# One step of a streaming encoder layer: the sample's right outputs by way of B22 and T3, P7 ahead of P6, a fifth raw place; in attention the sample's step third

## The chip, the cores and the metric

The kernel runs on one core of one Trainium2 chip, in one launch. The metric is the device time in microseconds; the time before is the median of three runs, 1524.59 us (1523.52 to 1526.95).

## The reference, cut to what matters

A prompt of 1024 rows (64 per chunk) and a sample of 64 rows with 2048 cached positions go through one layer:

```python
n = rms_norm(x, norm_attn_g); q, k, v (diff), q, k, v (stick) = split(n @ w_in)       # 1024 x 3072
s = q . k / 8 - slope[h] * |q_pos - k_pos|, visible where k_pos // 64 <= q_pos // 64   # 4 heads, 2 maps each
o_diff = rms(softmax(s[0]) @ v - lam * softmax(s[1]) @ v) * subln_g * (1 - lam_init)
z = q . k / 8; a = sigmoid(z) * prod of (1 - sigmoid(z)) over later visible k          # 8 heads of 64
h = x + concat(o_diff, a @ v) @ w_out
y = rms_norm(h + (silu(m @ w_gate) * (m @ w_up)) @ w_down, norm_final_g), m = rms_norm(h, norm_ffn_g)
```

D_MODEL is 1024 and the hidden width 2816, so w_down is 2816 x 1024. All is fp32. slope[h] is 2^-2, 2^-4, 2^-6, 2^-8. The outputs are y and the new k and v, for prompt and sample.

## The kernel before, in words

Each stage is a function with its own block, and each engine runs its own list of instructions in the order written; semaphores tie them. SP issues nearly all DMAs, in the order written, and a load that waits holds up those behind it. An fp32 matmul is made of three: both operands are split in a high and a low part (ScalarE or VectorE casts, VectorE or POOL subtracts), and high x high, high x low and low x high are accumulated.

Attention (`attend`). Eight units (four differential heads, then four pairs of stick-breaking heads) of SPU = 5 steps each, 40 steps x. In a unit four steps each take two prompt blocks of 128 rows (the p-th block and the (7-p)-th, nine blocks of keys together), one step takes the sample (2112 keys). Before, the sample's step is the fifth of each unit. In iteration i TensorE makes the scores of step i + 3, transposes the weights of step i and multiplies them with the values; for a stick-breaking step ScalarE takes sigmoids (L801), and VectorE makes the products with a scan over each row (`survive`, L977, for step i + 1), four scans for a prompt step, one of 2112 columns for the sample's. A group of four transpositions needs the scans of its rows. Every iteration also prepares pieces of the next unit's keys (L1080, L767, L868), and in stick-breaking units VectorE turns the values into differences of neighbours (`shift`, L989, seven pieces a unit, by the table `shift_at`). In iterations 32 to 37 VectorE casts the 16 pieces of w_out (L1000) and POOL subtracts their low parts (L747).

The distance tables: POOL's iota writes `near` (128 x 1024, L718) and `far` (128 x 2112, two of 64 rows, L722) as signed distances. VectorE takes the absolute value (L886 near, L892 far) and multiplies by 0.25 once for each differential unit (L899, L905). The far table's absolute value and first scaling stand at iteration 0, the near table's at iteration -5.

`mix` multiplies with w_out, adds x and norms. `feed` makes gate and up and multiplies them, in the hidden stage with seven products of half-sized matrices (L2233 to L2235), and then the down product, which this change is about.

Down product (in `feed`). The prompt's hidden values A (1024 x 2816) and w_down B are cut in 2 x 2 quarters: rows of A in two halves, the 2816 into even and odd tiles f of 128, columns of B in left and right. Seven products q = 0 to 6 of 512 x 1408 by 1408 x 512 are made, from sums of quarters of A (in `s_dram`, made by `sum_s`) and of B (in `t_dram`, by `sum_t`). Each result of four row blocks r (L2262 to L2264 in PSUM, six banks in turn) is added by VectorE to those of the four corners y11, y12, y21, y22 that it belongs to (`add_result`, L2128, table TAKEN_BY): two, four, one, one, three, two and one additions. An entry (q, k) is a 128 x 512 piece of A's sum and one of B's, for k of 11. Per entry SP loads both (L1801, L1810, 256 KB each) into one of RAWS = 4 raw places, ScalarE casts both (L1940, L1941), POOL makes A's low part (L1880), VectorE B's (`low_b`, L2109), in one of SLOTS = 12 slots. TensorE takes the k in three groups (4, 4, 3); in a group for each r three matmuls per k. A raw place is free when both low parts are done, a slot when the group of the entry 12 before is done by all r. From entry 10 on each entry's loads are followed by one of 16 loads of h (L1818, 256 KB), to which the corners are added.

The sample (64 rows) needs A times B in full. Its hidden values are loaded at once (`sample_raw`, 704 KB, at entry 14), split by ScalarE (L1945) and VectorE (L2113), and multiplied inside the products q = 1, 2 and 3, whose B pieces are B11, B21 and B22 as they are, ahead of the last r of each group (L2277 to L2281). B12 is in no product as it is, so before there are 11 half entries (EXTRA) with B12's rows and without A, placed behind each group of q = 1; they have two raw places of their own in the halves of `g_sb`, so that NE = 88 entries.

The final norms of the top half's four tiles and of the sample are placed at entries late in q = 5 (`norm_entry`), when y11 and y12 are complete; those of the bottom half come after the last product. The stores of y follow by SP.

## Time and profile before

| | |
|---|---|
| median of the runs | 1524.59 us |
| the profiled execution | 1528.52 us, its span 1526.7 us |
| TensorE busy | 1444.3 us (95%), granted clock 0.976 |
| VectorE, ScalarE, POOL busy | 896.1, 572.9, 492.7 us |
| DMA | 212.55 MB, mean 139 GB/s |

Times are from the start of the span. Attention goes from 312 to 667 us, the hidden stage to 1275.6, the down product from there to the end. Idle time of TensorE is what to read first; a busy TensorE is shown with matmuls whose ends overlap the next ones' starts, so the distance of starts is the measure.

### The profile page before, as it was taken

The numbers are of one execution on the slowest core, as the hardware profiler recorded it, in microseconds if no ns is written. First come the engines' busy times: TensorE is split into PE (matmuls) and PEld (weight loads), VectorE is DVE, ScalarE is ACT, GpSimd is POOL, SyncE is SP. The second block draws the span as 40 slices with busy tenths as digits, with TensorE's granted clock in tenths as the row PEclk, the third lists the DMA queues.
The fourth block names the chain that finished last, engine by engine and source line by source line (L and its number), as shares of the span: only waits on it lengthen the run. The fifth ranks groups of instructions, "written<-read, shape, count | busy, mean of one in ns | idle before, by whom it ended". The sixth has DMA issues, their size and how long they took to land. (4 is left out here: it accounts for less than half of the span.)

```text
span 1526.7 us, 24037 instructions
## 1 busy us (share of the span) xinstructions
PE 1444.3 (95%) x9360; PEld 1240.3 (81%) x9360; DVE 896.1 (59%) x1242; ACT 572.9 (38%) x1123; POOL 492.7 (32%) x376
## 2 busy tenths in 40 slices
PE   7999999969999999879968999999999999889998
PEld 6788888848887776558858999999999999668886
DVE  4520000078886787945558766666666677684484
ACT  4211111147877777522324222222222223444352
POOL 1323330010000001621225554444554445254453
PEclk9999999979999999979988999999999999999999
DMA  7243111163444555433312443344444346876563
GB/s 248 104 155 117 52 46 49 45 160 103 123 118 126 143 142 144 137 117 128 100 62 83 161 161 133 126 141 138 161 133 161 136 172 214 283 247 201 158 228 110
DMA packets 184871, 212.55 MB, mean 139 GB/s; under 512 B 19840, under 2 KB 126712, under 8 KB 183352
## 3 DMA queue, kind: packets, MB, share of 16 engines
q1 hardware_dynamic: 176136, 193.19, 39.4%
q10 hardware_dynamic: 8624, 17.83, 3.2%
q8 instruction: 75, 1.23, 0.3%
q14 instruction: 36, 0.29, 0.1%
HBM read 151.66 MB, written 59.31 MB: 138 GB/s over the span
## 5 line engine op out<-in xcount | busy, mean ns | idle before, releaser
L360 PE MATMUL ps_proj<-shared,nT_hi 128*128 128x512 f32 x384 | 152.6, 397 | 1.6 <-POOL shared L171 0.9
L361 PE MATMUL ps_proj<-shared,nT_hi 128*128 128x512 f32 x384 | 152.0, 396 | 0.0
L362 PE MATMUL ps_proj<-shared,nT_lo 128*128 128x512 f32 x384 | 150.6, 392 | 0.0
L268 DVE TENSOR_TENSOR staging<-ps_proj,staging 64x512 f32<-64x512 f32 x6 | 4.2, 694 | 214.5 <-ACT staging L203 214.5
L203 ACT COPY staging<-ps_proj 128x512 f32<-128x512 f32 (+1 forms) x54 | 31.7, 586 | 233.9 <-PE ps_proj L362 215.5
L1130 PE MATMUL ps_aT<-ident,z 128*128 128x128 f32 (+1 forms) x568 | 96.8, 287 | 6.4 <-DVE z L977 6.4
L810 ACT COPY aT<-ps_aT 128x512 f32<-128x512 f32 (+2 forms) x168 | 86.6, 524 | 33.0 <-PE ps_aT L1130 31.6
L171 POOL TENSOR_TENSOR shared<-w_raw,shared 128x512 fp32r<-128x512 f32 x40 | 59.4, 1521 | 112.9 <-DVE shared L241 112.9
L977 DVE TENSOR_TENSOR_SCAN z<-z,near 128x1024 f32<-128x1024 f32 (+7 forms) x64 | 92.1, 1485 | 0.0
L1875 POOL TENSOR_TENSOR shared<-staging,shared 128x512 fp32r<-128x512 f32 x43 | 64.4, 1503 | 85.6 <-ACT shared L1912 85.6
L1875 POOL TENSOR_TENSOR ring_more<-staging,ring_more 128x512 fp32r<-128x512 f32 x45 | 71.0, 1582 | 60.2 <-ACT ring_more L1912 60.1
L360 PEld LDWEIGHTS ps_proj<-shared,nT_hi 128*128 128x128 f32 x384 | 72.7, 189 | 19.5 <-POOL shared L171 2.2
L747 POOL TENSOR_TENSOR shared<-staging,shared 128x512 fp32r<-128x512 f32 x16 | 38.3, 2415 | 150.0 <-DVE shared L1000 150.0
L362 PEld LDWEIGHTS ps_proj<-shared,nT_lo 128*128 128x128 f32 x384 | 72.7, 189 | 16.2
L361 PEld LDWEIGHTS ps_proj<-shared,nT_hi 128*128 128x128 f32 x384 | 72.8, 190 | 14.7
L1130 PEld LDWEIGHTS ps_aT<-ident,z 128*128 128x128 f32 (+1 forms) x568 | 65.0, 143 | 23.2 <-issue 10.7
L2233 PE MATMUL ps_up<-parts_early,shared 128*128 128x272 f32 x264 | 77.1, 292 | 3.4 <-POOL shared L1875 3.4
L2233 PE MATMUL ps_up<-shared,ring_more 128*128 128x272 f32 x264 | 76.9, 291 | 3.3 <-DVE shared L2006 3.3
L1925 ACT COPY aux<-ps_up 128x544 f32<-128x544 f32 x22 | 13.5, 613 | 173.2 <-PE ps_up L2235 173.2
L2234 PE MATMUL ps_up<-parts_early,shared 128*128 128x272 f32 x264 | 77.1, 292 | 0.0
L2235 PE MATMUL ps_up<-parts_early,shared 128*128 128x272 f32 x264 | 76.8, 291 | 0.0
L2234 PE MATMUL ps_up<-shared,ring_more 128*128 128x272 f32 x264 | 76.8, 291 | 0.0
(298 smaller groups left out, 4477.1 us busy)
## 6 DMA issues: line engine op xcount, KB each, us to landing
staging<-s_dram SPq DMA_DIRECT2D x58, 256.0 KB, 3.5
staging<-in_w_gate SPq DMA_DIRECT2D x11, 1024.0 KB, 7.8
blocks<-in_w_up SPq DMA_DIRECT2D x11, 1024.0 KB, 5.3
blocks<-in_w_down SPq DMA_DIRECT2D x11, 1024.0 KB, 9.7
t_dram<-blocks SPq DMA_DIRECT2D x11, 1024.0 KB, 3.9
s_dram<-blocks SPq DMA_DIRECT2D x11, 1024.0 KB, 5.2
w_raw<-in_w_in SPq DMA_DIRECT2D x5, 2048.0 KB, 8.6
staging<-t_dram SPq DMA_DIRECT2D x34, 256.0 KB, 4.3
```

The lines of the kernel that those rows point to most:

```text
L171: nc.gpsimd.tensor_tensor(w_lo[g % 2][:, k], w_raw[:, g % 2, k], w_hi[g % 2][:, k].bitcast(F32), ALU.subtract).then_inc(w_lo_done, 1)
L360: nc.tensor.matmul(out, a_hi, b_hi, start=(k == 0), stop=False)
L361: nc.tensor.matmul(out, a_hi, b_lo, start=False, stop=False)
L362: last = nc.tensor.matmul(out, a_lo, b_hi, start=False, stop=(k == KD - 1))
L747: nc.gpsimd.tensor_tensor(t["wo_lo"][part], raw[:, slot_of(raw_of["wout", n])].rearrange("p a b -> p (a b)"), t["wo_hi"][part].bitcast(F32 ...
L810: last = nc.scalar.copy(aT[:, G % AT, 0:f], ps_aT[:, G % 2, 0:f])
L977: nc.vector.tensor_tensor_scan(back, back, mask[:, ::-1], 1.0, ALU.mult, ALU.max).then_inc(ready, 1)
L1130: last = nc.tensor.transpose(ps_aT[0:m, G % 2, k], z(x, at, m), t["ident"][:, :])
L1875: nc.gpsimd.tensor_tensor(w_lo, product_source(m)[0], w_hi.bitcast(F32), ALU.subtract).then_inc(w_lo_done, 1)
L2233: nc.tensor.matmul(res, w_hi[:, k], x_hi, start=(k == 0), stop=False)
L2234: nc.tensor.matmul(res, w_hi[:, k], x_lo, start=False, stop=False)
L2235: last = nc.tensor.matmul(res, w_lo[:, k], x_hi, start=False, stop=(k == HK - 1))
```

## The change

In attention the sample's step of a stick-breaking unit is the third of its unit instead of the fifth; those behind it are the third and fourth prompt step. The shift pieces come up to an iteration earlier. The absolute value of the distance tables is taken only where distances are negative (the last 128 columns of near, the last 64 of far), and the far table's first scaling moves from VectorE to POOL, behind the iotas.

In the down product the half entries go: NE = 77. The sample's right half is (A_even + A_odd) B22 + A_even (B12 - B22): the sum of the sample's even and odd tiles is made by VectorE into PSUM (`add_even_odd`), split like the rest, and multiplied in q = 3 (B22), and T3 = B12 - B22 (sign turned against before) is the B piece of the product now at q = 4. For this P7 stands at q = 4 and P6 at q = 5, so that y12 is complete only after q = 5, and the norms of the top tiles move into q = 6. g_sb is a fifth raw place for whole entries up to q = 4; then four places, and g is loaded at entry 59 instead of at q = 3's start. sample_raw is loaded at entry 10 instead of 14.

```diff
+    def sample_place(x):
+        return SPU - 1 if is_diff(x) else 2
     def is_sample(x):
-        return x % SPU == SPU - 1
+        return x % SPU == sample_place(x)
...
+        p = x % SPU - (1 if x % SPU > sample_place(x) else 0)
...
-            for j, i in enumerate((-2, -1, 0, 0, 1, 1, 2)):
+            for j, i in enumerate((-2, -1, -1, 0, 0, 1, 1)):
                 shift_at.setdefault(SPU * u + i, []).append((u, j))
...
+            pool.wait_ge(tables, 3)
+            nc.gpsimd.tensor_scalar(far[:], far[:], 0.25, 0.0, ALU.mult, ALU.add).then_inc(tables, 1)
...
             def near_distances():
-                nc.vector.scalar_tensor_tensor(near[:], near[:], -1.0, near[:], ALU.mult, ALU.max).then_inc(near_done, 1)
+                last = near[:, seq - P:]
+                nc.vector.scalar_tensor_tensor(last, last, -1.0, last, ALU.mult, ALU.max).then_inc(near_done, 1)
...
             def far_distances():
-                nc.vector.scalar_tensor_tensor(far[:], far[:], -1.0, far[:], ALU.mult, ALU.max).then_inc(far_done, 1)
+                last = far[:, past:]
+                nc.vector.scalar_tensor_tensor(last, last, -1.0, last, ALU.mult, ALU.max).then_inc(far_done, 2)
...
                     far_distances()
-                    far_slope(0)
...
-    SLOTS, RAWS, NBANK, AHEAD = 12, 4, 6, 10
+    SLOTS, RAWS, NBANK, AHEAD = 12, 5, 6, 10
+    entries = [(q, k) for q in range(NPROD) for k in range(NP)]
-    TAKEN_BY = (("y12", "y22"), ("y11", "y12", "y21", "y22"), ("y11",), ("y12",), ("y12", "y21", "y22"),
-                ("y21", "y22"), ("y21",))
+    TAKEN_BY = (("y12", "y22"), ("y11", "y12", "y21", "y22"), ("y11",), ("y12",), ("y21", "y22"),
+                ("y12", "y21", "y22"), ("y21",))
...
-            return last_group(4) + 6 + norm_order.index(i)
+            return last_group(5) + 6 + norm_order.index(i)
+        gains_at = entry_of[5, 0]
         def place(e):
-            return RAWS + k % 2 if q == EXTRA else (a_count[e] - 1) % RAWS
+            return e % RAWS if e < gains_at else (e - gains_at) % (RAWS - 1)
...
-            x = staging[:, s * D:(s + 1) * D] if s < 3 else aux[:, 0:D]
+            x = staging[:, s * D:(s + 1) * D] if s < 3 else aux[:, 0:D] if s == 3 else g_sb
...
-                if e == AHEAD + TT:
+                if e == AHEAD:
                     sp.dma_start(sample_raw, t["sample_dram"]).then_inc(sample_loaded, 16)
...
             def high_sample():
-                nc.scalar.copy(sample[:, :, 0:dec], sample_raw).then_inc(sample_hi_done, 1)
+                nc.scalar.copy(sample[:, 0:NF, 0:dec], sample_raw).then_inc(sample_hi_done, 1)
+                act.wait_ge(sample_summed, 1)
+                nc.scalar.copy(sample[:, NF:, 0:dec], sample_sum).then_inc(sample_hi_done, 1)
...
+            def add_even_odd():
+                nc.vector.tensor_tensor(sample_sum, pairs[:, :, 0], pairs[:, :, 1], ALU.add).then_inc(sample_summed, 1)
             def low_sample():
+                for j, (fs, x) in enumerate(((slice(0, NF), sample_raw), (slice(NF, None), sample_sum))):
...
                 low_b(e)
-                if e == SLOTS + 2:
+                if e == SLOTS + 1:
+                    add_even_odd()
+                if e == SLOTS + 3:
                     low_sample()
...
             def down_sample(q, k, j, first, final):
-                f = 2 * k + (1 if q in (2, 3) else 0)
+                f = (None, 2 * k, 2 * k + 1, NF + k, 2 * k)[q]
...
-                        if r == TT - 1 and q in (1, 2, 3):
+                        if r == TT - 1 and q in (1, 2, 3, 4):
...
-                                if q == 1:
-                                    down_sample(1, k, 0, k == 0, False)
-                                    down_sample(EXTRA, k, 1, k == 0, False)
-                                else:
-                                    down_sample(q, k, q - 2, False, k == NP - 1)
+                                down_sample(q, k, (q - 1) // 2, q % 2 == 1 and k == 0, q % 2 == 0 and k == NP - 1)
```

The rest of the diff follows from these: counts of semaphores without the half entries, A_PLACE and two signs (`sum_s`, `sum_t`) turned, the corners that the norms wait for.

## Rows read from the trace of the kernel before

**Rows 1.** Windows of the down product: busy us (instructions) of each engine, clock, DMA share, GB/s.

```profile
1362.60:1519.30 156.70, 156.70 (x691) 128.19 (x689) 88.10 (x91) 64.46 (x114) 76.38 (x63) 1.00 0.56 181
```

**Rows 2.** Timeline of TensorE: start, us, line, operation, [idle before <- releaser].

```profile
1275.61 0.39 PE L2262 MATMUL ps_up<-parts_early 128*128 128x512 f32 x1
...
1299.39 0.47 PE L2262 MATMUL ps_up<-shared 128*128 128x512 f32 x1 [0.47 <-DVE shared L2109]
...
1359.27 0.77 PE L2262 MATMUL ps_up<-shared 128*128 128x512 f32 x1 [2.35 <-DVE shared L2109]
...
1519.09 0.39 PE L2264 MATMUL ps_up<-parts_early 128*128 128x512 f32 x1
```

**Rows 3.** Chain that ended last, 1355 to 1362: start, length of the piece.

```profile
1360.89 0.43 PE ps_up L2262
```

**Rows 4.** Waits of TensorE in the down product: us, times, longest.

```profile
PE ps_up L2262 <- DVE shared L2109: 7.9, 7, 2.4
```

**Rows 5.** Timeline of SP's queue, first half of the down product.

```profile
1302.66 0.65 SPq L1818 DMA_DIRECT2D blocks<-h_dram  x1
1312.02 0.33 SPq L1810 DMA_DIRECT2D g<-in_w_down  x1
...
1329.41 0.33 SPq L1810 DMA_DIRECT2D g<-in_w_down  x1
```

**Rows 6.** Timeline of VectorE in the down product.

```profile
1305.97 1.37 DVE L2109 TENSOR_TENSOR parts_early<-staging,parts_early 128x512 fp32r<-128x512 f32 x1 [0.59 <-ACT parts_early L1941]
1308.57 1.63 DVE L2113 TENSOR_TENSOR part_late<-blocks,part_late 128x1408 fp32r<-128x1408 f32 x1 [1.22 <-ACT part_late L1945]
...
1355.76 2.47 DVE L2128 TENSOR_TENSOR blocks<-ps_up,blocks 128x512 f32<-128x512 f32 x4
...
1470.73 4.08 DVE L2146 SCALAR_TENSOR_TENSOR blocks<-blocks,rstd,g 128x1024 f32<-128x1024 f32 x1
...
1477.63 2.39 DVE L2109 TENSOR_TENSOR parts_early<-staging,parts_early 128x512 fp32r<-128x512 f32 x2
```

**Rows 7.** The tile far: operations, duration ns min/median/max, first and last start.

```profile
L905 DVE TENSOR_SCALAR far<-far x4: 1249/1250/1260, 339.4 to 437.3; 128x2112 f32<-128x2112 f32 x4
...
L977 DVE TENSOR_TENSOR_SCAN z<-z,far x4: 4542/4543/4544, 517.0 to 653.1; 128x2112 f32<-128x2112 f32 x4
L722 POOL IOTA far<- x2: 1889/1890/1891, 313.0 to 314.9; 64x2112 f32 x2
...
L892 DVE SCALAR_TENSOR_TENSOR far<-far x1: 2349/2349/2349, 337.0 to 337.0; 128x2112 f32<-128x2112 f32 x1
L734 POOL MEMSET far<- x1: 1857/1857/1857, 467.7 to 467.7; 128x2112 f32 x1
```

**Rows 8.** Timeline of TensorE in attention.

```profile
342.77 0.58 PE L1110 MATMUL ps_z<-shared 64*128 64x256 f32 x2 [3.84 <-DVE lowest L933]
...
650.46 1.12 PE L1130 MATMUL ps_aT<-ident,z 128*128 128x128 f32 x4 [5.54 <-DVE z L977]
```

**Rows 9.** Timeline of ScalarE at attention's end.

```profile
664.51 0.31 ACT L828 ACTIVATE o_sb<-ps_o,v_last 128x64 f32<-128x64 f32 x1 [0.83 <-PE ps_o L1159]
```

**Rows 10.** Timeline of ScalarE in the down product: casts behind their loads.

```profile
1298.69 0.62 ACT L1940 CAST shared<-aux 128x512 fp32r<-128x512 f32 x1 [0.85 <-DMA aux<-in_w_down]
...
1304.80 0.63 ACT L1940 CAST parts_early<-staging 128x512 fp32r<-128x512 f32 x1 [0.82 <-DMA staging<-in_w_down]
...
1307.16 1.37 ACT L1945 CAST part_late<-blocks 128x1408 fp32r<-128x1408 f32 x1 [1.22 <-DMA blocks<-sample_dram]
```

**Rows 11.** Groups of the down product, POOL: busy us, mean ns.

```profile
L1880 POOL TENSOR_TENSOR parts_early<-staging,parts_early 128x512 fp32r<-128x512 f32 x30 | 42.7, 1424 | 43.8 <-ACT parts_early L1940 43.7
```

**Rows 12.** The tile near: scalings.

```profile
L899 DVE TENSOR_SCALAR near<-near x4: 681/682/916, 316.4 to 422.7; 128x1024 f32<-128x1024 f32 x4
```

**Rows 13.** Groups by form, VectorE: 470 to 600, then 603 to 658.

```profile
L977 DVE TENSOR_TENSOR_SCAN z<-z,near 128x1024 f32<-128x1024 f32 x6 | 13.4, 2269 | 0.0
...
L977 DVE TENSOR_TENSOR_SCAN z<-z,near 128x1024 f32<-128x1024 f32 x2 | 6.6, 3325 | 0.0
```

More of the change, by code:

```diff
@@ L1544, in feed @@
     NG = len(GROUPS)
[L1545 to L1553 removed]
+    SLOTS, RAWS, NBANK, AHEAD = 12, 5, 6, 10
+    entries = [(q, k) for q in range(NPROD) for k in range(NP)]
     NE = len(entries)
[L1555 to L1558 removed]
+    TAKEN_BY = (("y12", "y22"), ("y11", "y12", "y21", "y22"), ("y11",), ("y12",), ("y21", "y22"),
+                ("y12", "y21", "y22"), ("y21",))
+    A_PLACE = (2, 0, 1, 5, 4, 3, 6)
     entry_of = {what: e for e, what in enumerate(entries)}
[L1560 removed]
     def steps_until(q, k):
[L1564 removed]
+        return (q * NG + k // 4 + 1) * TT
     def summed(name, q, r):
@@ L1662, in feed @@
             old = user_before(e)
-            raw_landed[e] = (0 if old is None else raw_landed[old]) + (16 if q == EXTRA else 32)
+            raw_landed[e] = (0 if old is None else raw_landed[old]) + 32
         def slot(e):
@@ L1702, in feed @@
         s_stored = sem("s_stored")
-        raw_loaded = [sem(f"raw_loaded4{i}") for i in range(RAWS + 2)]
+        raw_loaded = [sem(f"raw_loaded4{i}") for i in range(RAWS)]
         a_hi_done = sem("a_hi_done")
@@ L1792, in load_entry @@
                     old = user_before(e)
-                    if q != EXTRA:
-                        sp.wait_ge(a_lo_done, a_count[old])
+                    sp.wait_ge(a_lo_done, old + 1)
                     sp.wait_ge(b_lo_done, old + 1)
@@ L1797, in load_entry @@
                 landed = raw_loaded[place(e)]
-                if q != EXTRA:
-                    sp.wait_ge(hidden_stored, 48 * (k + 1))
-                    sp.wait_ge(s_stored, 16 * (k + 1))
-                    sp.dma_start(a_raw, t["s_dram"][A_PLACE[q], k]).then_inc(landed, 16)
+                sp.wait_ge(hidden_stored, 48 * (k + 1))
+                sp.wait_ge(s_stored, 16 * (k + 1))
+                sp.dma_start(a_raw, t["s_dram"][A_PLACE[q], k]).then_inc(landed, 16)
                 rows = [t["w_down"][f * P:(f + 1) * P] for f in (2 * k, 2 * k + 1)]
@@ L1806, in load_entry @@
                     sp.wait_ge(t_stored, 16 * (k + 1))
-                src = (t_even[:, left], rows[0][:, left], rows[1][:, left], rows[1][:, right], t_odd[:, right],
-                       t_even[:, right], t_odd[:, left], rows[0][:, right])[q]
+                src = (t_even[:, left], rows[0][:, left], rows[1][:, left], rows[1][:, right], t_even[:, right],
+                       t_odd[:, right], t_odd[:, left])[q]
                 sp.dma_start(b_raw, src).then_inc(landed, 16)
@@ L1889, in _ @@
             for e, (q, k) in enumerate(entries):
-                if q != EXTRA:
-                    low_a(e)
+                low_a(e)
                 for c, i in enumerate(norm_order[:TT + 1]):
@@ L1938, in high @@
                 a_hi, _, b_hi, _ = slot(e)
-                if q != EXTRA:
-                    nc.scalar.copy(a_hi, raw(e)[0]).then_inc(a_hi_done, 1)
+                nc.scalar.copy(a_hi, raw(e)[0]).then_inc(a_hi_done, 1)
                 nc.scalar.copy(b_hi, raw(e)[1]).then_inc(b_hi_done, 1)
@@ L2201, in _ @@
                         add_result(q, r)
-                    if q == 3 and r == TT:
+                    if q == 4 and r == TT:
                         add_sample()
```

53 lines of the change are left out of this document (21 added, 32 removed).

## The prediction

> **What bounds the kernel now.** I read the page's busy line, then TensorE's waits by stage, then TensorE's timeline, then the queue and engine feeding each wait. TensorE is the bound; other engines matter where it waits. A microsecond taken from such a wait comes off the end if TensorE is busy from there on.
>
> Down product: TensorE does 7 x 11 x 4 x 3 = 924 matmuls and 11 x 4 x 2 = 88 for the sample, 1012. In the last 156.7 us it never waits: 156.70 us for 691, a spacing of 0.2268 us [rows 1]. The first of the 1012 starts at 1275.61, the last at 1519.09 [rows 2], so 243.5 us pass for 1011 spacings, which would need 229.3: 14.2 us are lost. All are lost before 1362.6. One is the wait for the eleventh entry (1299.39, idle 0.47), 0.6 us beyond its spacing. The longest is at 1359.27, idle 2.35, and behind it six matmuls come 0.43 apart [rows 2, 3], the 1.2 GHz level, for 1.2 us more. VectorE's low parts (L2109) end them: 7.9 us of idle in 7 waits [rows 4]; the restart behind each makes up much of the rest.
>
> What makes the low parts late: SP issues in order. At 1302.66 it has issued two of the half entries (the 11 loads of B12's rows, EXTRA) into their two places; the third waits for the first's low part until 1312.02 [rows 5]. For 9.4 us nothing is loaded, the full entries behind least of all. The same happens again up to 1329.41. Then q = 1's four-corner additions, 2.47 us per row block, fall between low parts that are already late at 1355.76 [rows 6], and give the two waits at 1356 to 1359.
>
> Attention, start: VectorE makes the far table at 337.0, 2.35 us absolute value (L892) and 1.25 us scaling (L905), with score reads queued behind; TensorE idles 3.84 us up to 342.77 for a bank [rows 7, 8]. Attention, end: VectorE's scans bound. TensorE idles 5.54 us up to 650.46; the last scan starts at 653.1 and takes 4.54; the last output starts at 664.51 [rows 7 to 9].
>
> **The change part by part. Half entries.** Off go 11 loads of 256 KB, 11 casts, 11 low parts; TensorE's count stays 1012. The two long pauses of SP go with their places. Loads can then be four to five entries ahead instead of blocked. I place what is late next:
> - Eleventh entry: its load waits for the last stored sums, as before; 0.6 us stays.
> - q = 1 starts at 1306.3 (1275.61 + 132 x 0.2268 + 0.7 of the first wait) and needs its fourth entry (e = 14) 9 matmuls later, at 1308.3. Before, e = 11 landed at 1298.7 and e = 14 at 1304.80, 2.04 us each (with the h load); the sample's 704 KB came behind, and with one h load (960 KB) took 2.36 [rows 10]. Now they go ahead of e = 11: 704/960 x 2.36 = 1.7 us later, so e = 14 lands at 1306.5. Casts to 1307.6. Low part 1.37 at 1305.97 [rows 6], and the new addition add_even_odd (128 x 704) stands ahead of it, which is nearest to half of the 1408 wide difference of 1.63: 0.8, behind e = 13 at 1307.4, so to 1308.3. Done at about 1309.7: wait 1.4. Bounds: 0 (addition inside the casts' time, the extra raw place brings loads forward), 2.4 (addition behind a POOL operation of 1.42 [rows 11]).
> - Sample's parts: needed 36 matmuls after the start, 1306.3 + 1.4 + 8.2 = 1315.9. Behind e = 14 on VectorE: an addition of two corners (half of 2.47), e = 15 (1.4), differences 1.63 + 0.8: 1314.8, or 1316.2 with one POOL operation ahead. 0.2 taken, bounds 0 and 1.
> - e = 18, with three more additions of two corners (1.24) and low parts (up to 1.37) ahead: about 1323.0 against a need at 1322.5. 0.4 taken, bounds 0 and 1.5.
> - q = 1 to 2: the additions (2.47 x 4) now stand at e = 23 to 26. With T the start of q = 2, the first row block is ready at T - 7.5, added by T - 5.0; each further pair (1.37 + 2.47) brings e = 24 to T - 3.6, e = 25 to T + 0.3 against a need at T + 2.0. Nothing, bound 1.5.
> - Half-clock stretch: goes, as no wait reaches 2.35.
> Left: 0.6 + 1.4 + 0.2 + 0.4 = 2.6 of 14.2, and 0.6 for restarts: **11.0 us** gained, bounds 7 (all upper bounds) and 12.9 (0.6 and 0.7 left).
>
> **P7 ahead of P6.** Three-corner additions move from q = 4 to 5, and the norms of the top rows from q = 5 to 6, with their stores. Nothing is added to the end: those rows follow the same adds in the same pattern. In q = 5 before, that pattern kept VectorE full (one norm took 4.08 us beside POOL), yet q = 5's last low parts ended at about 1478.7 to 1480 from 1470.73 and 1477.63 [rows 6], and q = 5 starts at 1519.3 - 2 x 29.9 = 1459.5, so its last entry is needed 23.2 later, at 1482.7. Slack near 4 us. Five y stores, 2.3 MB, in the last product end before its 29.9 us do. Cost 0, bound 2. Signs, A_PLACE and the gain's place and load: same instructions, 0. The fifth place ends at q = 5; q = 2 to 6 never waited with four.
>
> **Tables.** The far absolute value covers 64 columns instead of 2112 (0.2 instead of 2.35), and the first scaling (1.25) leaves VectorE: 3.4 us off a wait of 3.84, TensorE near full behind it. **3.4** taken; 1 if TensorE's next dependence (the combine's weights) comes right behind. The near absolute value loses 1.0 us or so, but the scaling behind it took 0.92 against 0.68 for its sisters while POOL's iota ran to 316.8 [rows 7, 12], and it would wait for that iota still: 0 taken, bounds 0 and a gain of 0.5. POOL's new scaling of 2112 columns lies between the memset of as many (1.86) and four differences of 512 (4 x 1.42 = 5.7) [rows 7, 11]; nearest to the memset, 2 to 3 us at 316.9 to 320, its reader comes 30 us later. Cost 0.
> The row shows a VectorE scaling held up while POOL runs. The Trainium skill says why, in SBUF - State Buffer, section "SBUF: two separate sides": VectorE and GpSimd share a port pair, and whoever starts first has it for the whole instruction. By that rule the new POOL scaling, if it starts ahead of near_slope, holds it for its whole length; the trace agrees so far as 0.92 against 0.68 goes.
> For that scaling the Trainium skill's GPSIMD Engine Reference, section "3.1 Elementwise", gives 1.03 cycles an element for light bodies, an estimate of 1.8 us; the sum would be the same.
>
> **Sample third, shifts earlier.** In the last unit the last step becomes a prompt step. VectorE is bound from about 606. Its scans from x = 34 on: before 4.5 + 4 x 5.3 + 4.5; after one of the two sample steps is a prompt step of about 5.3: +0.8. POOL's differences of w_out delay scans by 1.05 each (1024 wide: 3.33 against 2.27) but not the sample's (4.54 always) [rows 7, 13]; the sample's scan now meets others of them, +1 to +2, and the raw places behind it come free later, +0.5. One wait of VectorE for a w_out load (1.6) may go. Last scan ends 1.5 later. Then before, five groups of transpositions follow the scan: 664.51 - 657.6 = 6.9 us to the output; after, two of five groups go ahead of the last scans, 3/5 x 6.9 = 4.1 plus the lag, about 5, so 1.9 less. Sum **0.5** gained; bounds: lost 4.5 (all of the delays, 3 more for the clock at its lower level behind a longer wait), gained 4 (delays vanish). In units 4 to 6 the order costs 0: TensorE has no wait there that the step's place would change.
>
> **Sum:** 11.0 + 3.4 + 0.5 = 14.9. The profiled execution took 1528.52 (span 1526.7, 1.8 around it), 3.9 above the median 1524.59; 1528.52 - 14.9 = 1513.6, against the median **1509.7 us**.
>
> **The rivals.**
> B, arrivals bound q = 1. For: DMA moved 256 KB per 0.68 us just there, with no pause to spare, and 704 KB now go first; if an entry takes 2.7 us, e = 14 is ready at 1311.7, and waits of 3.4 and about 2 with a stretch at the lower clock (1.2) are left: with the first wait and restarts 7.8 of 14.2. Against: 2.8 MB fewer. Gain 6.4 + 3.9 = 10.3: 1514.3.
> C, attention's end gets longer by its bound, 4.5: 14.9 - 0.5 - 4.5 = 9.9: 1514.7. For: VectorE has no pause there; against: the shorter tail.
> D, the order pays 4 there: 18.4: 1506.2.
> E, POOL's scaling gets the pair before near_slope: near_slope ends 2 to 5.7 later and TensorE with it, 3 taken: 1512.7. Against: near_slope is there first.
> F, slower: the norms in the last product. They stand on VectorE ahead of its last low parts. If all five take the 4.08 of the slow one, 2.8 x 5 = 14 more, 10 beyond the slack, and the last 36 matmuls at 0.43 instead of 0.227 add 7.3: 17.3 against 14.9 gained, 1527.0. It decides from the point where the last low part comes 14.9 us of such loss after need; it speaks for it that VectorE was full there, against it that before this pattern cost TensorE nothing.
> G, the change doesn't do what it says: the waits move to the next entries unchanged, as the low parts themselves and not SP's pauses are the bound; 11 low parts and casts less at most. Gain 3.4 + 2 = 5.4: 1519.2.
>
> **How the numbers follow.** Forecast 0.50, B 0.15, C 0.12, D 0.10, E 0.04, F 0.03, G 0.06. Range 1505 to 1519: it takes in B, C, D, E and G's edge, and leaves about 2 in 10 outside. What a measurement of this kernel can tell from no change is 0.2%, 3 us. Faster: all but F and part of what I have not thought of, 0.94; same 0.02; slower 0.04.
>
> **What would show it.** Right: no pause over 3 us of SP between 1300 and 1325 (in its own time), TensorE's waits in the down product together under 3 us, the longest by e = 14 at q = 1's start, no matmuls 0.43 apart; the wait of 3.84 near 342 under 0.6; q = 6 without a wait though VectorE is full; from the last scan's end to the last output about 5 us. Wrong: waits for L2109 over 5 us in all (B, G), a scan end in attention more than 4 us later against its start (C), near_slope over 2 us (E), a wait in the last product (F).

## The result, and the profile after

The changed kernel took 1511.85 us (median of 4 runs, 1510.37 to 1513.51) beside 1524.83 us for the kernel before: ratio 0.9914, interval 0.9897 to 0.9931, 13.0 us faster. Timed again (e5 below) it stood at 0.9896, 0.9878 to 0.9913. Forecast were 1509.7 and 14.9 us. The profiled execution took 1510.37 us (span 1508.3). Gains given for the experiments are worked out from their ratios. One of the five runs of e3 was a slow one (1550.26 us, granted clock 0.91) and is left out of its time and ratio.

I cut both traces at the same places, each the start of an instruction (the last scan: its end): TensorE's first instruction of attention and of the mix stage (both are transpositions, made by matmuls), the first and last scan, and the first and last matmul of the down product. All kernels measured below are in the same table, us:

| kernel | attention's first matmul to first scan | scans | last scan's end to mix stage's first matmul | mix stage | down product, first to last matmul |
|---|---|---|---|---|---|
| before | 168.2 | 177.6 | 14.3 | 129.2 | 243.5 |
| after | 162.5 | 180.2 | 14.4 | 126.2 | 231.1 |
| e1 new down product alone | 168.0 | 177.7 | 13.2 | 126.4 | 230.9 |
| e2 four half places | 168.7 | 177.5 | 14.0 | 126.0 | 235.4 |
| e3 new tables alone | 162.2 | 177.6 | 14.3 | 126.1 | 242.4 |
| e4 sample fifth | 162.2 | 177.7 | 13.4 | 127.8 | 231.4 |
| e5 changed kernel again | 162.2 | 179.1 | 15.2 | 129.2 | 231.3 |
| e6 four raw places | 162.2 | 183.3 | 13.8 | 128.2 | 232.3 |
| e7 sample fourth | 162.2 | 176.3 | 15.2 | 126.1 | 231.2 |
| e8 sample fifth, its parts later | 164.1 | 177.6 | 14.6 | 126.3 | 230.5 |
| e9 double work | 163.0 | 185.9 | 14.4 | 125.8 | 239.0 |
| e10 more bytes | 161.3 | 179.0 | 14.9 | 128.0 | 234.4 |
| e11 combined | 164.0 | 176.3 | 15.3 | 128.0 | 230.3 |

The hidden stage (from the end of the mix stage to the down product), whose code is the same in all but for two signs, takes 473.2 to 474.5. Between the two profiled executions: 5.7 from the tables, 12.4 from the down product, 2.8 lost in the scans and their hand-over, 3.0 in the mix stage, whose code did not change, and 0.2 ahead of all: 5.7 + 12.4 - 2.8 + 3.0 + 0.2 = 18.5, where the spans differ by 18.4. The 3.0 is most of the distance to the medians' 13.0, and is no effect of the change: the changed kernel's own mix stage took 126.2 in one execution and 129.2 in another (e5). What differs is the granted clock (third column from the end) in one stretch, 100 to 110 us into the stage, here before and after:

```profile
771.88:781.88 10.00, 9.25 (x32) 7.69 (x33) 1.30 (x2) 1.17 (x2) 0.00 (x0) 0.66 0.01 2
```
```profile
768.82:778.82 10.00, 9.44 (x45) 7.44 (x46) 1.80 (x3) 2.23 (x4) 0.65 (x2) 1.00 0.13 50
```

It is 1.00 there in the seven executions whose mix stage took 125.8 to 126.4, 0.83 in the four with 127.8 to 128.2 and 0.66 in the two with 129.2.

**Down product.** TensorE's timeline, first and last matmul and the only wait, against [rows 2, 3]; its waits there against [rows 4]; and the window from that wait on against [rows 1]:

```profile
1269.58 0.39 PE L2275 MATMUL ps_up<-parts_early 128*128 128x512 f32 x1
...
1301.35 0.39 PE L2277 MATMUL ps_up<-parts_early 128*128 128x512 f32 x1
1302.80 0.47 PE L2275 MATMUL ps_up<-parts_early 128*128 128x512 f32 x1 [1.07 <-DVE parts_early L2112]
...
1500.66 0.39 PE L2277 MATMUL ps_up<-parts_early 128*128 128x512 f32 x1
```
```profile
PE ps_up L2275 <- DVE parts_early L2112: 1.1, 1, 1.1
```

Before, beside the seven waits of [rows 4], there were two more, one of 0.8 us and this one:

```profile
PE ps_up L2280 <- DVE shared L2109: 1.1, 1, 1.1
```

After, from the one wait on:

```profile
1302.80:1500.90 198.10, 198.10 (x871) 160.95 (x871) 114.88 (x130) 78.31 (x140) 94.31 (x76) 1.00 0.58 190
```

Of nine waits (9.8 us) one is left, and from 1302.80 to the last matmul TensorE never stops. It waits for entry e = 14. ScalarE's and VectorE's timeline about it (against [rows 6, 10]):

```profile
1299.64 0.62 ACT L1941 CAST parts_early<-g 128x512 fp32r<-128x512 f32 x1 [0.89 <-DMA g<-in_w_down]
```
```profile
1300.08 0.89 DVE L2119 TENSOR_TENSOR ps_up<-blocks 128x704 f32<-128x704 f32 x1
1300.88 1.77 DVE L2112 TENSOR_TENSOR parts_early<-g,parts_early 128x512 fp32r<-128x512 f32 x1
...
1305.07 2.71 DVE L2124 TENSOR_TENSOR part_late<-blocks,part_late 128x1408 fp32r<-128x1408 f32 x1
...
1309.69 1.74 DVE L2112 TENSOR_TENSOR parts_early<-staging,parts_early 128x512 fp32r<-128x512 f32 x1
```

e = 14 lands late; the addition (L2119) takes 0.89 and ends 0.2 us after the second cast, so it puts the low part off by little. The low part is long, though: 1.77 us, where e = 13's took 1.37. SP's queue, against [rows 5]:

```profile
1306.05 0.43 SPq L1820 DMA_DIRECT2D blocks<-h_dram  x1
1311.49 0.32 SPq L1803 DMA_DIRECT2D staging<-s_dram  x1
```

One pause of 5.0 us is left (from the end of one issue to the start of the next; the 9.4 of before, taken from start to start, is 8.7 by this measure), where I had said none over 3: the load of e = 21 waits for the low part of e = 16, which stands behind the sample's differences of 2.71 at 1305.07. TensorE does not notice, since five entries lie ahead. In the last product one of five norms took the long form and TensorE had no wait:

```profile
1482.22 4.07 DVE L2157 SCALAR_TENSOR_TENSOR blocks<-blocks,rstd,g 128x1024 f32<-128x1024 f32 x1
...
1488.02 0.67 DVE L2112 TENSOR_TENSOR parts_early<-staging,parts_early 128x512 fp32r<-128x512 f32 x1
```

The last low part ends at 1488.7; its first reader starts 29 spacings of 0.2268 before the last matmul, at 1494.1: 5.4 us of slack.

**Tables.** The tile far, against [rows 7], near's scaling, against [rows 12], and TensorE's wait, against [rows 8]:

```profile
L914 DVE TENSOR_SCALAR far<-far x3: 1249/1250/1251, 358.4 to 431.4; 128x2112 f32<-128x2112 f32 x3
...
L729 POOL TENSOR_SCALAR far<-far x1: 2287/2287/2287, 316.7 to 316.7; 128x2112 f32<-128x2112 f32 x1
L902 DVE SCALAR_TENSOR_TENSOR far<-far x1: 213/213/213, 336.9 to 336.9; 128x64 f32<-128x64 f32 x1
```
```profile
315.30 1.84 DVE L909 TENSOR_SCALAR near<-near 128x1024 f32<-128x1024 f32 x1
```
```profile
339.30 0.39 PE L1118 MATMUL ps_z<-shared 64*128 64x256 f32 x2 [0.44 <-DVE lowest L942]
```

near_slope starts 1.1 us sooner, lasts 1.84 instead of 0.92 and ends at 317.14, before at 317.36: it waited for GpSimd's iota (which ends at 316.6) from inside instead of in front, and gains nothing. The wait of 3.84 is 0.44. What I had not counted shows in the granted clock of the windows behind it, first before (and the stretch at the lower level), then after:

```profile
340.00:345.00 5.00, 2.23 (x12) 2.03 (x13) 4.86 (x15) 0.88 (x3) 0.00 (x0) 0.68 0.14 44
345.00:350.00 5.00, 5.00 (x27) 3.89 (x25) 2.50 (x8) 2.18 (x7) 0.00 (x0) 0.64 0.04 12
342.00:348.50 6.50, 5.73 (x26) 4.56 (x27) 4.29 (x16) 1.08 (x3) 0.00 (x0) 0.50 0.00 0
```
```profile
340.00:345.00 5.00, 5.00 (x38) 3.99 (x38) 4.76 (x17) 3.94 (x12) 0.00 (x0) 1.00 0.32 97
345.00:350.00 5.00, 5.00 (x38) 4.49 (x38) 4.87 (x14) 4.88 (x15) 0.00 (x0) 1.00 0.78 220
```

Before, the clock was at 1.00 from 338.5 to 341.5, then fell to 0.50, the 1.2 GHz level, while TensorE still waited, and TensorE worked on at that level: full, but with 27 instead of 38 matmul instructions in 5 us. An estimate from these rows: the 5.7 us of work up to 348.5 at half the clock cost 2.9 us. The two traces leave 2.3 for it: 5.7 gained, less 3.4 of wait.

**Sample third.** VectorE's timeline in unit 5 (the second of the stick-breaking units 4 to 7), and TensorE's:

```profile
539.22 4.55 DVE L986 TENSOR_TENSOR_SCAN z<-z,far 128x2112 f32<-128x2112 f32 x1
543.68 0.43 DVE L884 SCALAR_TENSOR_TENSOR shared<-ps_z,shared 64x64 fp32r<-64x64 f32 x2
544.13 0.23 DVE L886 TENSOR_TENSOR shared<-ps_z,shared 128x64 fp32r<-128x64 f32 x1
```
```profile
544.50 0.50 PE L1118 MATMUL ps_z<-kT_hi,qT_hi 64*128 64x512 f32 x2 [1.77 <-DVE shared L886]
```

The sample's scan, 4.55 us long, now falls just where the next unit's small key piece is to be split, ahead of it on VectorE, and TensorE waits 1.77. It does so once in each of three units (1.50, 1.77 and 1.77), 5.0 us together. Unit 5's first scan comes at 519.02 and unit 6's at 563.82: 44.8 us, where the kernel before takes 43.2. From the first scan of all to the first scan of step 34 it takes 130.3 us instead of 126.7, and from there to the end of the last scan 49.9 instead of 50.9. And at attention's end, ScalarE's last output (against [rows 9]) and SP's queue:

```profile
659.85 0.63 ACT L843 ACTIVATE o_sb<-ps_o,v_last 128x128 f32<-128x128 f32 x2 [0.88 <-PE ps_o L1171]
```
```profile
659.16 0.33 SPq L372 DMA_DIRECT2D staging<-mixed  x1
659.54 0.43 SPq L373 DMA_DIRECT2D staging<-mixedT  x1
660.02 0.97 SPq L692 DMA_DIRECT2D mixedT<-o_sb  x2
661.16 0.34 SPq L372 DMA_DIRECT2D staging<-mixed  x1
661.54 0.49 SPq L373 DMA_DIRECT2D staging<-mixedT  x1
662.07 0.98 SPq L692 DMA_DIRECT2D mixedT<-o_sb  x2
```

The last scan ends at 654.38 and the last output starts 5.5 later instead of 6.9, as forecast; but its store is issued 2.2 after it, behind loads that waited for GpSimd's last low part of w_out (four of them took 15.69 us, up to 659.14, among the scans).

### The profile page after: what moved, and what is told of

Its sections match the earlier page's. It is cut to its first block and busy times, and to the rows that moved or that the text cites. A ratio compares the mean times of both kernels' runs of the same rounds, so it can differ in the third digit from the quotient of the medians.

```text
span 1508.3 us, 23998 instructions
## 1 busy us (share of the span) xinstructions
PE 1435.4 (95%) x9360; PEld 1236.0 (82%) x9360; DVE 880.0 (58%) x1232; ACT 566.3 (38%) x1113; POOL 501.3 (33%) x377
## 5 line engine op out<-in xcount | busy, mean ns | idle before, releaser
L753 POOL TENSOR_TENSOR shared<-staging,shared 128x512 fp32r<-128x512 f32 x16 | 43.3, 2734 | 151.5 <-DVE shared L1009 151.5
L1878 POOL TENSOR_TENSOR shared<-staging,shared 128x512 fp32r<-128x512 f32 x43 | 64.4, 1503 | 85.6 <-ACT shared L1914 85.6
L360 PEld LDWEIGHTS ps_proj<-shared,nT_hi 128*128 128x128 f32 x384 | 72.6, 189 | 19.5 <-POOL shared L171 2.2
```

Of the source, the lines that this page charges most:

```text
L360: nc.tensor.matmul(out, a_hi, b_hi, start=(k == 0), stop=False)
L1878: nc.gpsimd.tensor_tensor(w_lo, product_source(m)[0], w_hi.bitcast(F32), ALU.subtract).then_inc(w_lo_done, 1)
```

## The experiments

**e1: the new down product alone.** Attention's function is taken whole from the kernel before.

> The kernel before with only the new down product; attention is that of the kernel before. By the prediction's terms the down product gives 11.0 us and the rest of the 14.9 is attention's. The two traces put the down product at 12.5 us (from its first matmul to its last 243.5 before, 231.1 after). Theory (the gain is the down product's): 11 to 12.5 us under the kernel before, about 1512.5 to 1513.5 beside a kernel before of 1524.8, that is, hardly above the whole change; its down product has a single wait, near 1 us, for the entry e = 14. Rival (attention carries a third or more of the 13.0 us): 1516 or more, which can only be if the down product's own length differs from 231.

1513.12 us, ratio 0.9918 (0.9905 to 0.9930): 12.5 us faster. Down product 230.9, its one wait:

```profile
PE ps_up L2267 <- DVE parts_early L2104: 0.9, 1, 0.9
```

So nearly all of the 13.0 is the down product's. Attention's edits together gave 0.6 us by the changed kernel's first timing and 3.4 by its second (0.9914 and 0.9896 against 0.9918), neither clear of the intervals, and 2.9 by the traces (5.7 less 2.8); they were forecast at 3.9.

**e2: is it SP's pauses, or the half entries' work?**

```diff
-            return RAWS + k % 2 if q == EXTRA else (a_count[e] - 1) % RAWS
+            return RAWS + k % 4 if q == EXTRA else (a_count[e] - 1) % RAWS
+        g_more = h_all[:, NT - 1]
-                elif e == AHEAD + 4 * TT:
+                elif e == AHEAD + 4 * TT + 11:
+                    sp.wait_ge(b_lo_done, entry_of[2, 0])
```

> The kernel before with the half entries kept (11 loads of 256 KB, 11 casts, 11 low parts, TensorE's work as before) but with four places for them instead of two, so that SP's queue need not stand behind the third and fourth half entry of a group (the two new places lie in the sample's rows of h, which are loaded 11 entries later). Theory (SP's pauses are the cause, the work and the bytes are not): most of the down product's gain is there without the change: 8 to 12 us faster than before, no pause of SP over 3 us between the third and fourth half entry, TensorE's waits for the low parts under 3 us. Rival G (the low parts and casts themselves are the bound): 0 to 3 us faster, TensorE's waits for the low parts still 5 us or more. Rival of bytes (2.8 MB more through the DMA engines in the 70 us that are at 288 GB/s after the change, 9.8 us of transfer at that rate): 0 to 4 us faster, with waits of ScalarE's casts for landings in place of the pauses.

1515.85 us, ratio 0.9937 (0.9925 to 0.9949): 9.6 us faster with all the half entries still there. Down product 235.4 against 242.4 to 243.5. SP's queue over the first group of halves (every second load; the h loads between are left out), then TensorE's waits:

```profile
1297.40 0.43 SPq L1813 DMA_DIRECT2D g<-in_w_down  x1
...
1298.48 0.51 SPq L1813 DMA_DIRECT2D g<-in_w_down  x1
...
1299.58 0.50 SPq L1813 DMA_DIRECT2D blocks<-in_w_down  x1
...
1300.61 0.43 SPq L1813 DMA_DIRECT2D blocks<-in_w_down  x1
```
```profile
PE ps_up L2266 <- DVE shared L2113: 3.8, 4, 2.2
```

The four loads go out in 3.6 us instead of standing up to 9.4. Two places more give 7 to 8 of the 11 to 12 us: the queue's order was the larger cause, and G falls as the main one. The waits that stay are 4.0 us (3.8 and one of 0.2 beside it), more than the 3 that the theory allowed, and 4.2 us of down product, which went only with the halves.

**e3: the tables alone.** The kernel before with the new attention function, but the sample fifth everywhere and the old table of shifts.

> The kernel before with only the two distance tables changed: absolute values over 64 columns of far and 128 of near, the first scaling of far on GpSimd. The prediction's term: 3.4 us faster, the wait of 3.84 us near 342.8 down to under 0.6. What the two traces suggest instead: 5.8 us at the start of attention, because the wait was followed by some 7 us of matmuls at a granted clock of 0.64 to 0.68, which go with it. Of these some may be given back by the end of attention, where VectorE is the bound only in the last units. So 3.4 (1521.4) by the term, 5 to 6 (1519) by the clock, with the granted clock at 1.00 in the 10 us from 340 on; 0 if the stick-breaking phase eats it.

1520.26 us, ratio 0.9961 (0.9948 to 0.9974): 5.9 us faster, and 6.0 in the trace (168.2 to 162.2). Its window behind the wait that went:

```profile
340.00:345.00 5.00, 5.00 (x38) 4.01 (x38) 4.74 (x17) 3.94 (x12) 0.00 (x0) 1.00 0.36 102
```

The wait's 3.4 and what stood behind it, 2.6, both come through to the end; the scans' length stays 177.6. The clock was not changed by itself, so the split in two is by the windows and not by a run.

**e4: the sample fifth again.**

```diff
     def sample_place(x):
-        return SPU - 1 if is_diff(x) else 2
+        return SPU - 1
-            for j, i in enumerate((-2, -1, -1, 0, 0, 1, 1)):
+            for j, i in enumerate((-2, -1, 0, 0, 1, 1, 2)):
```

> The changed kernel with the sample's step back in fifth place in units 4 to 7, and the shifted pieces of v at their old iterations; tables and down product as changed. The prediction: sample third gains 0.5 net, so this kernel would be 0.5 slower than the changed one, about 1512.4. Rival (read from the traces: the sample third loses 2.7 us of lead between the first stick-breaking scan and the last, by waits of TensorE in units 4 to 6, and 1 us at SP's queue at the end, against 2.2 us saved behind the last scan): this kernel is 1 to 2 us faster than the changed one, about 1510. In its trace the last scan would end near 652 and the mix stage's first matmul come near 667 to 668 instead of 668.8.

1506.67 us, ratio 0.9872 (0.9859 to 0.9885): about 5 us faster than the changed kernel (3.7 against its 0.9896, 6.4 against its 0.9914). The gains add up: e1's 12.5 and e3's 5.9 are 18.4, and this kernel, which has both edits, gains 19.5. VectorE's first scans of units 5 and 6:

```profile
516.90 4.46 DVE L986 TENSOR_TENSOR_SCAN z<-z,near 128x1024 f32<-128x1024 f32 x2
...
560.12 4.46 DVE L986 TENSOR_TENSOR_SCAN z<-z,near 128x1024 f32<-128x1024 f32 x2
```

43.2 us a unit again. The sample's third place costs; it does not pay. From here on my theory of that edit was the rival's.

**e5: the changed kernel once more**, beside the next three.

> The changed kernel once more, beside the next three on one chip, as their measure. By its earlier timing 0.9914 of the kernel before (13 us). If the kernel with the sample fifth (0.9872) was faster than this one by its own doing and not by the session, this one stays at 0.990 to 0.992 here, that is 5 to 7 us slower than that one; if the session made it, 0.987 to 0.989. The two profiled executions so far differ by only 2.9 us.

1508.26 us, ratio 0.9896 (0.9878 to 0.9913). At the edge of what the theory asked; its two timings lie 2.4 and 4.2 parts in a thousand above e4's 0.9872, and neither interval contains that, though e4's own (up to 0.9885) and this one (from 0.9878) overlap a little. The sign rests on the traces as much as on the timing. Its scans took 179.1, the hand-over 15.2.

**e6: four raw places.**

```diff
-    SLOTS, RAWS, NBANK, AHEAD = 12, 5, 6, 10
+    SLOTS, RAWS, NBANK, AHEAD = 12, 4, 6, 10
-            return e % RAWS if e < gains_at else (e - gains_at) % (RAWS - 1)
+            return e % RAWS
```

> The changed kernel with four raw places instead of five (the buffer of the final gain stays empty until the gain is loaded). Theory (the gain comes from the half entries' pauses, the fifth place only adds slack): the same time as the changed kernel within 1 us, or up to 2 us slower through a longer wait at the start of q = 1, since a load then waits for the low part of the entry four before it. Rival (the fifth place carries the gain, because the loads run one entry further ahead): 4 us slower or more, with several waits of TensorE for the low parts in q = 0 to 2.

1512.11 us, ratio 0.9916 (0.9901 to 0.9931): 3.0 us slower than e5, outside the expected 2, but the intervals overlap and the trace gives most of it to the scans (183.3 against 179.1), where nothing was edited. Its down product is 232.3, about 1 longer, by a second wait, the first of these two:

```profile
1296.85 0.47 PE L2275 MATMUL ps_up<-shared 128*128 128x512 f32 x1 [0.76 <-DVE shared L2112]
1307.30 0.47 PE L2275 MATMUL ps_up<-parts_early 128*128 128x512 f32 x1 [1.34 <-DVE parts_early L2112]
```

The fifth place is worth about 1 us: mostly the eleventh entry's wait, which I had left standing at 0.6. The rival's 4 us or more is not in the down product.

**e7: the sample fourth**, `return SPU - 1 if is_diff(x) else 3`, shifts as changed.

> The changed kernel with the sample's step fourth instead of third in units 4 to 7. In the traces units 5 and 6 last 43.2 us each with the sample fifth (as in the kernel before) and 44.8 with it third: TensorE waits 1.7 to 1.8 for the last key pieces' low parts, which the sample's scores need two steps earlier. Theory: the need of those pieces moves with the step, so that fourth is early enough by one step: units of 43.2 and no such wait; the last unit ends with one prompt step of 640 and hands over as with the sample third. Then 3 to 5 us faster than the changed kernel, level with the sample fifth or 1 us ahead. Rival (the long scan in mid unit is what costs, whichever place): units of 44.8, no faster than the changed kernel.

1506.76 us, ratio 0.9887 (0.9869 to 0.9905): 1.4 us faster than e5 by timing, not told apart from it, where 3 to 5 were expected. By the trace it is 2.7 from the first scan to the mix stage's first matmul (191.6 against 194.3). Scans 176.3, the shortest; unit 5 takes 43.6, though unit 4 still 44.8:

```profile
518.59 4.46 DVE L986 TENSOR_TENSOR_SCAN z<-z,near 128x1024 f32<-128x1024 f32 x2
...
562.16 4.46 DVE L986 TENSOR_TENSOR_SCAN z<-z,near 128x1024 f32<-128x1024 f32 x2
```

The table of shifts is as in the changed kernel, so it is not what costs. The three waits for L886 are gone, and three of 0.51 for other key pieces stand there; that fits the long scan's meeting with the key piece. What was gained against the sample fifth (e4) in the scans, 1.4 us, is given back in the hand-over (15.2 against 13.4).

**e8: the sample fifth, and its parts behind entry 14.**

```diff
-                if e == AHEAD:
+                if e == AHEAD + 4:
                     sp.dma_start(sample_raw, t["sample_dram"]).then_inc(sample_loaded, 16)
-                if e == SLOTS + 1:
+                if e == SLOTS + 2:
                     add_even_odd()
```

> The changed kernel with the sample fifth, and in the down product the sample's 704 KB loaded after entry 14 instead of after entry 10, its even-odd addition after the low part of entry 14. Theory (the only wait left, 1.07 us for the low part of e = 14, 1.2 with its restart, is a matter of arrival: the sample's bytes went ahead of the entry): the wait falls to under 0.3, and the down product to 229.9 us; against the kernel with the sample fifth (1506.7 beside a kernel before of 1526.4) 1 us faster, ratio 0.986 to 0.987. Rival (arrival is not it, VectorE's and GpSimd's long low parts there, 1.77 and 1.76 us, are): the wait stays near 1 us. If the sample's parts come too late instead, a wait of 0.5 to 1.5 us stands in front of its first matmul.

1504.81 us, ratio 0.9864 (0.9848 to 0.9880). TensorE's only wait of the down product is now for the sample's parts:

```profile
1306.98 0.50 PE L2288 MATMUL ps_up<-shared,part_late 128*128 128x512 f32 x1 [0.23 <-DVE part_late L2124]
```

The wait for e = 14 is gone. The edit moves the load and the addition together, but the trace tells them apart. Counted from the first matmul of the down product, e = 14's casts start 28.2 us in, where they started 30.1 in with the changed kernel: 1.8 earlier by arrival, more than the whole wait of 1.07. And its low part is short again:

```profile
1297.88 1.36 DVE L2112 TENSOR_TENSOR parts_early<-g,parts_early 128x512 fp32r<-128x512 f32 x1 [0.68 <-ACT parts_early L1942]
```

1.36 instead of 1.77, and 0.1 less delay: 0.5 us were the addition's and the long low parts', the rival's share. So it was in the main arrival behind the sample's 704 KB, as the prediction's working had it. The down product takes 230.5, 0.9 less than e4's; the timing can't tell 0.9 us.

**e9: the half entries' work without their loads.**

```diff
+                if q == 1:
+                    nc.scalar.copy(b_hi, raw(e)[1]).then_inc(b_hi_done, 1)
+                    act.wait_ge(b_hi_done, b_count[e] - 1)
                 nc.scalar.copy(b_hi, raw(e)[1]).then_inc(b_hi_done, 1)
```

and the same for VectorE's low part.

> The changed kernel with the half entries' work put back without their loads and places: in q = 1 each of the 11 entries' right operand is cast twice by ScalarE and its low part made twice by VectorE (same values, each repeat behind its first). The kernel before with four half places won 7 to 8 of the down product's 12 us (243.5 or 242.4 to 235.4); 4 are left, with four waits for low parts, the longest 2.2. Theory (the 4 are the work: 1.4 us of VectorE for each half entry where VectorE is late anyway): down product 3 to 4.5 us longer than the changed kernel's 231.2, 234 to 236, with waits for low parts of 3 us. Rival (the 4 are the 2.8 MB of transfers): down product 231 to 232.

1519.10 us, ratio 0.9940 (0.9920 to 0.9959). Down product 239.0, 7.8 longer, more than either theory said. Waits, and the window they lie in:

```profile
PE ps_up L2282 <- DVE parts_early L2119: 2.5, 2, 1.4
PE ps_up L2282 <- DVE shared L2119: 2.3, 1, 2.3
```
```profile
1300.00:1330.00 30.00, 24.98 (x93) 18.88 (x92) 29.06 (x32) 20.32 (x35) 16.82 (x12) 0.89 0.80 271
```

VectorE is busy 29.06 of 30 us, TensorE waits 4.8 and the granted clock falls to 0.89. Of the 7.8 longer, 3.8 are waits (4.9 of idle instead of 1.1) and 3.4 are two rows of eight matmuls 0.43 us apart, behind the second and the third wait. The run overstates the halves' work, since here each repeat delays its own entry from the first one of q = 1 on, whereas a half entry was needed 36 matmuls into the step. What it shows is that VectorE has no room in these 30 us.

**e10: the half entries' bytes without their work.**

```diff
                 load_entry(e)
+                if entry_of[1, 0] <= e < entry_of[3, 0]:
+                    j = e - entry_of[1, 0]
+                    if j >= 3:
+                        sp.wait_ge(extra[j % 3], 16 * (j // 3))
+                    sp.dma_start(g_sb[:, j % 3 * 256:j % 3 * 256 + 256],
+                                 t["w_down"][j * P:(j + 1) * P, 0:256]).then_inc(extra[j % 3], 16)
```

> The changed kernel with four raw places and, beside each of the 22 entries of q = 1 and q = 2, a further load of 128 KB into the empty buffer (2.8 MB, the half entries' bytes, without their work). The kernel with four raw places had a down product of 232.3 us. Theory (work and pauses, not bytes): 232 to 233. Rival (bytes): 235 to 236, with waits of ScalarE's casts for landings and of TensorE for low parts in q = 1.

1511.52 us, ratio 0.9908 (0.9886 to 0.9929). Down product 234.4, 2.1 above e6's: between the two theories. e = 14 waits 1.55 and an entry 2.5 us before it 0.79, 2.3 us of idle against e6's 2.1 (0.76 and 1.34, 10.5 us apart). The rest is the granted clock behind the second of the two waits:

```profile
1300.00:1310.00 10.00, 8.34 (x29) 6.47 (x30) 9.46 (x11) 6.44 (x11) 6.63 (x4) 0.83 1.06 381
```

In e6 it is 1.00 in the same ten microseconds; here eight matmuls stand 0.43 apart, 1.7 us lost. So the bytes lengthen the waits by 0.2 us and put them close together, and that costs the 2. Of the 4.2 us that four half places left, bytes can account for some 2 and work for the rest; the two runs don't split them more finely, their sum isn't additive, and the further loads also take SP's time to issue, which no run separates.

**e11: a version to beat both.** e7 and e8 together, and SP's order at attention's end:

```diff
-                if i == NSTEP - 1:
+                if i == NSTEP:
...
-                if i >= NSTEP - 1:
...
-                    load_mixed(t, sp, i - NSTEP + 1)
+                    load_mixed(t, sp, 0)
```

with load_mixed(t, sp, 1) moved into the mix stage, behind the gains.

> A version meant to beat both kernels: the changed kernel with the sample's step fourth, its parts in the down product loaded and added behind entry 14, and at the end of attention SP's queue storing step 38 ahead of the first loads of the mix stage, the second of these loads left to the mix stage. From the traces: stick-breaking 176.3 instead of 179 to 183 us, hand-over from the last output to the first product of the mix stage 7 to 8 instead of 8.8 to 10.4, down product 230.5 instead of 231.2. Against the changed kernel (0.990 of the kernel before) 5 us faster: ratio 0.986 to 0.9875, about 1504. Against the sample fifth with late sample parts (0.9864) 0 to 2 us faster. Rival: the mix stage's second tile comes late by its load and takes the hand-over's gain back; then mix stage 127 instead of 126.1 and no gain against that kernel.

1505.37 us, ratio 0.9862 (0.9847 to 0.9877): 21 us faster than the kernel before and some 5 faster than the changed one, level with e8. Scans 176.3 and down product 230.3 as expected, but the hand-over stayed at 15.3. SP issued the last store 0.8 after the last output instead of 2.2, and then the first tile itself came late, by the load that had been moved back:

```profile
662.11 0.69 DVE L1377 TENSOR_TENSOR staging<-staging 128x512 f32<-128x512 f32 x1 [10.50 <-DMA staging<-mixedT]
```

## Why the prediction came out near, and where it was wrong

The total was near because two errors of opposite sign cancelled: forecast 11.0 + 3.4 + 0.5 = 14.9; the traces have 12.4 + 5.7 - 2.8 = 15.3, and with the mean of all executions for the last two terms 12.4 + 6.0 - 4.5 = 13.9.

- **Half entries, 11.0: measured 12.4.** The cause held (e2). Of the 2.6 left, the first wait of 0.6 went with the fifth place (e6: 1.1 without it); e = 14 was put at 1.4 of wait and measured 1.07 (1.2 with its restart: 1301.35 to 1302.80 is 1.45, less one spacing), in later executions 0.9 to 1.4; the sample's parts and e = 18 cost nothing, where 0.6 was set. Landing order made e = 14 late (1.8 us), and the addition and the long low parts 0.5 (e8), where I had given the addition 0.8 alone. With the restarts 3.2 of the 14.2 had been left, and 1.8 were. The 7.9 us of waits before were 9.8: two more stood outside the group that I read.
- **"No pause over 3 us of SP" was wrong**, 5.0, and harmless: five entries were in hand. Before it was 8.7 by the same measure (9.4 from start to start) and came again up to 1329.41 [rows 5], because four half loads shared two places and each group needed two round trips.
- **G** had the wrong main cause but was right in part: work and bytes of the half entries are 4 of the 12 us (e2; e9 and e10 show that each can make waits there). I had priced them at 2.
- **P7 ahead of P6, F: 0, held.** The one long norm was 4.07 and left 5.4 us of slack; 4 had been worked out for the product before.
- **near_slope and E: 0, held.** GpSimd's scaling took 2.29, started 1.4 us behind near_slope, and nothing waited for it. The Trainium skill's GPSIMD Engine Reference, section "3.1 Elementwise", gave an estimate of 1.8 us; the measured 2.29 decides. Its first 0.46 us lie beside near_slope, which ends at 317.14, and 1.83 are left behind that; that near_slope held it up so long was not tried by a run.
- What the Trainium skill says in SBUF - State Buffer, section "SBUF: two separate sides", that whoever starts first keeps the shared port pair for its whole instruction, agrees with near_slope's 1.84: it was held until the iota ended at 316.6 and then needed about 0.5.
- **Far table, 3.4: measured 5.7 to 6.0.** The mis-sized term: it took the wait itself and not the lower clock behind it, 2.3 to 2.6 us. I had seen that effect in the down product, where I counted it, and not looked at the windows behind this one.
- **Sample third, 0.5 gained: measured 2.8 lost in the profiled pair.** From the first scan to the mix stage's first matmul it takes 190.9 to 192.2 us, 191.6 on the mean, in eight executions with the sample fifth or fourth, and 194.7, 194.3, 197.1, 200.3 and 193.9 with it third, 196.1 on the mean: 4.5 us lost. The step that failed is the sentence "In units 4 to 6 the order costs 0: TensorE has no wait there that the step's place would change". TensorE had none because VectorE did the key pieces in time; I looked at TensorE's waits and not at what the moved 4.5 us scan would stand in front of on VectorE. The three waits for L886 are 5.0 us; from the first scan to that of step 34 it took 3.6 us longer in the profiled pair and 2.3 to 5.0 in the other four. "Last scan ends 1.5 later" was off to both sides: from step 34 on the scans took 0.8 to 1.0 less than the 50.9 before in three executions and 3.3 more in two (e6, e9). The tail behind the last scan came near the forecast (5.5 against "about 5"), but the hand-over took it back. C had the loss (4.5, 2.8 in the pair and 4.5 on the mean), but put it at attention's end, where only e6 and e9 have it; what the other three lost stood in units 4 to 6, a mechanism C didn't name.

That the total came near, 13.0 for 14.9, is therefore in part luck: the half entries' term was right in its mechanism, and the far table's shortfall covered a loss that I had forecast as a gain.

What stays open: why the scans with the sample third take 179.0 to 185.9 in executions of the same code, when the other orders repeat within 0.2. The differences arise in the last two units (but for 1.3 us of e9 in unit 5), where GpSimd's low parts of w_out and VectorE's scans stretch each other (a sample scan is 4.54 or 5.62 there, 640 columns 5.09 or 6.12 for four); that this is the cause wasn't tried.

## What to carry to other kernels

When a long instruction is moved, look on its own engine for the short ones it will now stand in front of, and who waits for those; the bound engine's waits before the change don't show them. A queue that issues in order is paid for by the place that comes free last, so count round trips per place against the time in which the group is used up, before counting the work. And price a wait of TensorE together with the granted clock in the windows behind it.

## What the runs showed of the hardware

- Taking away a wait of 3.84 us gave 5.9 in timing and 6.0 in the trace (e3). With the wait the granted clock had been at 0.50 for 6.5 us, from 342.0 to 348.5, after 1.00 from 338.5 to 341.5; without it it was 1.00 over the ten microseconds from 340 on.
- Shorter waits did this too. Two close together, 0.79 and 1.55, 2.5 us apart (e10), or 1.35 and 1.19, 2.1 us apart (e9), and one of 2.32 alone (e9) were each followed by some eight matmuls 0.43 us apart. A single wait of 1.4 (e4, e5), 0.65 and 2.25, 3.2 us apart (e2), or 0.76 and 1.34, 10.5 us apart (e6), left the clock at 1.00.
- The mix stage took 125.8 to 126.4 us in seven executions and 127.8 to 129.2 in six, with no edit in it but for one load in e11. The granted clock 100 to 110 us into it was 1.00 in the seven and 0.66 or 0.83 in the six. A difference of 3 us between two profiled executions says nothing before such a stretch has been looked at.
- Next to VectorE's scans a GpSimd difference of 512 columns took 3.9 us on the mean (4 in 15.69), where it takes 1.3 in the down product when it starts ahead of VectorE's.
